# Chunked attention run by pairs of heads on the two halves of the TensorE array, its first pairs between the query products

## The chip, the cores and the metric

The kernel runs on one core of one Trainium2 chip. The metric is the device time of one execution in microseconds (us). Before the change three runs gave 1208.13, 1211.26 and 1212.42 us, median 1211.26. One further execution was profiled; its trace is what this document reads. About 0.3% (3.6 us) is what a measurement of this kernel can tell from no change.

The engines are named as the profile names them: PE is TensorE's matmuls, PEld its weight loads, DVE VectorE, ACT ScalarE, POOL GpSimd, SP the engine that issues the weight loads from memory.

## What is computed

Two blocks of two layers each on a sequence of 256 tokens of width 1024, all in float32. The change touches the attention of the second block's second layer, and two small places of the other two attentions:

```
def chunked_mixer(h, k_band, v_band, w_q, rel_table, w_o):
    q = (h @ w_q).reshape(B, n_c, CHUNK, B_HEADS, B_HEAD_DIM)      # 16 heads of 64
    ...
    s = jnp.einsum('bnqhd,bnkhd->bnhqk', q, k_band, preferred_element_type=jnp.float32)
    s = s * (B_HEAD_DIM ** -0.5) + bias[None, None]
    ...
    p = jax.nn.softmax(s, axis=-1).astype(v_band.dtype)
    o = jnp.einsum('bnhqk,bnkhd->bnqhd', p, v_band).reshape(B, S, B_HEADS * B_HEAD_DIM)
    return o @ w_o
```

It is followed by `x = x + rms_norm_2(y, attn_post_g)`, another norm, and the gated MLP of 2816 columns. The order of the whole is: attention with 8 heads of 128 (called `moba` in the kernel), MLP, pooling layer, MLP, latent attention with 8 heads (`mla`), gated MLP, shared keys and values, chunked attention with 16 heads (`chk`), gated MLP.

## The kernel before

**Weights.** Every weight matrix is cut into chunks of 128 x 2048 (1 MB). `AT` gives the first chunk of each matrix: `bq` are the four of the chunked attention's query weights, `bwo` the four of its output weights, `ffn1` those of the gated MLP behind it. There are four slots. For each chunk, in order: SP loads it (`raw`), ACT rounds it (`whi`, line 596, `hi_part`), DVE subtracts (`wlo`, line 854, `lo_part`), PE uses it. `hi_part` waits until PE is done with the chunk that was last in the slot (`w_used` above `PREV`). A product is three matmuls, on lines 1306, 1307 and 1308: rounded by rounded, and each rounded part by the other's rest. Activations are split in the same way into `act_hi` (ACT) and `act_lo` (DVE).

**Order.** Each engine has one program, written out by hand; semaphores tie them together. `hi_before(c)` and `lo_before(c)` convert all chunks whose slot was last held by a chunk before `c`. Inside the attention loop the function `due` says after which head one whole chunk is converted.

**Chunked attention.** First the four chunks of the query product, `tiles_out` into PSUM banks 4 and 5 in turn, 48 matmuls each, copied and scaled by DVE (line 1282) to `qT`. Heads 2j and 2j+1 lie in rows 0 to 63 and 64 to 127 of `qT[:, j]`. Then `attention(chk, ...)` goes head by head. On PE, for head h:

- **scores**: two matmuls (128 and 256 keys, line 1705) that use the 64 rows of one head, into bank 4 or 5; each is carried out as two instructions;
- **turn**: head h-2's probabilities are transposed, three matmuls into bank 6 (line 1428);
- **values**: head h-3, two matmuls (lines 1443 and 1444) that fill 64 columns of the array, into one half of the partitions of bank 7;
- **output**: from h = 5 on, half of one pair's output product (`head_out`, one token tile): six matmuls of 128x512. Banks 0 and 1 gather the first token tile, 2 and 3 the second.

DVE takes the maximum (`tensor_tensor_reduce`, line 1014, with the bias added), ACT the exponential (line 652), DVE normalizes (line 1027), ACT copies the transposed probabilities (line 640) and the head outputs (line 646), DVE splits them (line 1034, semaphore `o_lo`). `keep_busy` puts matmuls on constants between the first heads (`BUSY[chk]` = 1, 2, 1, 5), as it does in the phases in which PE waits for a norm. POOL loads each head's bias from memory and multiplies it by 8 (line 491); heads 8 to 15 reuse the buffers of heads 0 to 7, one after the other, once DVE has taken their maxima.

**The end of an attention.** The last two pairs' output products are made together by `rows_out`, 24 matmuls, quarter by quarter. After two quarters the first token tile is complete: `post_stats` has ACT sum its squares (line 609), then DVE scales (line 983) and adds it to x (line 987), multiplies by the next gain (line 942), and PE transposes the result (`turn("fpre1")`, line 1342).

## Time and profile before

| | us |
|---|---|
| three runs | 1208.13, 1211.26, 1212.42; median 1211.26 |
| the profiled execution, its own time | 1212.48 |
| its span, first to last instruction | 1210.7 |
| PE busy | 1154.4 (95%) |
| DVE busy | 676.7 (56%) |
| ACT busy | 530.9 (44%) |

The time of an execution is the span and 1.8 us around it. "PEclk" is the clock granted to TensorE as a share of full speed: 1.00 is 2.4 GHz, 0.50 is 1.2 GHz. The profile models the ends of matmuls, so that two following matmuls overlap on paper; how long a row of matmuls takes is read from start to start. The chain of work follows the last instruction back to whatever released it, and so tells which engine sets the time in each stretch.

### The profile page before, as it was taken

The numbers are of one execution on the slowest core, as the hardware profiler recorded it, in microseconds if no ns is written. First come the engines' busy times: TensorE is split into PE (matmuls) and PEld (weight loads), VectorE is DVE, ScalarE is ACT, GpSimd is POOL, SyncE is SP. The second block draws the span as 40 slices with busy tenths as digits, with TensorE's granted clock in tenths as the row PEclk, the third lists the DMA queues.
The fourth block names the chain that finished last, engine by engine and source line by source line (L and its number), as shares of the span: only waits on it lengthen the run. The fifth ranks groups of instructions, "written<-read, shape, count | busy, mean of one in ns | idle before, by whom it ended". The sixth has DMA issues, their size and how long they took to land.

```text
span 1210.7 us, 17821 instructions
## 1 busy us (share of the span) xinstructions
PE 1154.4 (95%) x7132; PEld 1019.1 (84%) x7132; DVE 676.7 (56%) x933; ACT 530.9 (44%) x640; POOL 43.5 (4%) x69
## 2 busy tenths in 40 slices
PE   4999899999999999997898999999999999999997
PEld 4887799999889999977677999999888668999996
DVE  4745554455665544566545655555845556554554
ACT  5446344344443443444444443345433455344342
POOL 0000000000000000000000000002300410000000
PEclk9999999999999999998899999999999899999999
DMA  9751445645535556455313565556653222556550
GB/s 350 250 186 56 154 158 189 207 169 178 191 99 195 170 190 205 145 136 191 105 35 104 174 195 180 180 191 209 207 191 136 62 91 66 178 174 200 181 173 35
DMA packets 127450, 196.37 MB, mean 162 GB/s; under 512 B 7392, under 2 KB 97632, under 8 KB 127280
## 3 DMA queue, kind: packets, MB, share of 16 engines
q1 hardware_dynamic: 124256, 186.29, 46.6%
q0 software_dynamic: 3152, 9.51, 2.6%
q8 instruction: 28, 0.46, 0.2%
q14 instruction: 14, 0.11, 0.0%
HBM read 194.73 MB, written 1.05 MB: 162 GB/s over the span
## 4 chain that ended last, share of the span: by engine, by line
PE 84%; DVE 10%; ACT 3%; issue 1%; DMA 1%; DVEq 0%; SPq 0%; ACTq 0%
PE ps L1306 26%; PE ps L1307 25%; PE ps L1308 25%; DVE wlo L854 2%; DVE xs L942 1%; ACT whi L596 1%; PE ps L1443 1%; PE ps L1705 1%; PE ps L1428 1%; ACT junk L609 1%; DMA raw<-attn_w_qkv_in 1%; DVE act_lo L956 1%; PE ps L1664 1%; PE ps L1328 1%; DVE x L987 1%
## 5 line engine op out<-in xcount | busy, mean ns | idle before, releaser
L854 DVE TENSOR_TENSOR wlo<-raw,whi 128x2048 fp32r<-128x2048 f32 (+2 forms) x176 | 395.9, 2266 | 182.1 <-ACT whi L596 181.7
L1306 PE MATMUL ps<-act_hi,whi 128*128 128x256 f32 x1384 | 392.6, 284 | 7.7 <-DVE act_lo L956 4.7
L1307 PE MATMUL ps<-act_lo,whi 128*128 128x256 f32 x1384 | 391.7, 283 | 0.0
L1308 PE MATMUL ps<-act_hi,wlo 128*128 128x256 f32 x1384 | 391.6, 283 | 0.0
L596 ACT ACTIVATE whi<-raw 128x2048 fp32r<-128x2048 f32 (+2 forms) x176 | 328.8, 1888 | 118.6 <-PE ps L1308 104.0
L1306 PEld LDWEIGHTS ps<-act_hi,whi 128*128 128x128 f32 x1384 | 263.6, 190 | 12.5 <-issue 9.6
L1307 PEld LDWEIGHTS ps<-act_lo,whi 128*128 128x128 f32 x1384 | 263.6, 190 | 2.0
L1308 PEld LDWEIGHTS ps<-act_hi,wlo 128*128 128x128 f32 x1384 | 263.7, 191 | 0.0
L1308 PE MATMUL ps<-whi,hlo 128*128 128x512 f32 x400 | 156.8, 392 | 0.0
L1307 PE MATMUL ps<-wlo,hhi 128*128 128x512 f32 x400 | 156.8, 392 | 0.0
L1306 PE MATMUL ps<-whi,hhi 128*128 128x512 f32 x400 | 156.2, 390 | 0.0
L1306 PE MATMUL ps<-whi,act_hi 128*128 128x512 f32 (+2 forms) x286 | 112.8, 394 | 9.2 <-DVE act_lo L956 5.5
L1307 PE MATMUL ps<-wlo,act_hi 128*128 128x512 f32 (+2 forms) x286 | 109.1, 381 | 0.0
L1308 PE MATMUL ps<-whi,act_lo 128*128 128x512 f32 (+2 forms) x286 | 108.9, 381 | 0.0
L1053 DVE TENSOR_TENSOR arena<-arena 128x512 f32<-128x512 f32 x32 | 22.2, 692 | 132.4 <-ACT arena L668 132.4
L1308 PEld LDWEIGHTS ps<-whi,hlo 128*128 128x128 f32 x400 | 75.2, 188 | 16.0
L668 ACT ACTIVATE arena<-ps 128x512 f32<-128x512 f32 x32 | 19.1, 598 | 156.3 <-PE ps L1308 156.3
L1306 PEld LDWEIGHTS ps<-whi,hhi 128*128 128x128 f32 x400 | 75.2, 188 | 14.7
L1307 PEld LDWEIGHTS ps<-wlo,hhi 128*128 128x128 f32 x400 | 75.1, 188 | 14.6
L1306 PEld LDWEIGHTS ps<-whi,act_hi 128*128 128x128 f32 x286 | 54.7, 191 | 21.5 <-issue 8.3
L1308 PEld LDWEIGHTS ps<-whi,act_lo 128*128 128x128 f32 x286 | 54.6, 191 | 10.1
L1307 PEld LDWEIGHTS ps<-wlo,act_hi 128*128 128x128 f32 x286 | 54.9, 192 | 8.5
(157 smaller groups left out, 906.6 us busy)
## 6 DMA issues: line engine op xcount, KB each, us to landing
raw<-mlp_w_up_in SPq DMA_DIRECT2D x32, 1024.0 KB, 6.3
raw<-mlp_w_down_in SPq DMA_DIRECT2D x32, 1024.0 KB, 4.9
raw<-ffn_w_gate_in SPq DMA_DIRECT2D x22, 1024.0 KB, 5.4
raw<-ffn_w_up_in SPq DMA_DIRECT2D x22, 1024.0 KB, 5.3
raw<-ffn_w_down_in SPq DMA_DIRECT2D x22, 1024.0 KB, 4.8
raw<-attn_w_qkv_in SPq DMA_DIRECT2D x12, 1024.0 KB, 8.6
raw<-w_kv_shared_in SPq DMA_DIRECT2D x8, 1024.0 KB, 6.7
raw<-attn_w_o_in SPq DMA_DIRECT2D x4, 1024.0 KB, 4.8
```

Of the source, the lines that this page charges most:

```text
L596: nc.scalar.activation(whi[:, s, 0:width], raw[:, s, 0:width], ACT.Copy).then_inc(hi_ready, 1)
L609: nc.scalar.activation(junk[:, col * HALF:col * HALF + width], src, ACT.Square, accum_out=norm_stat(name, t, 0, col, col + 1)).then_inc(sq ...
L668: nc.scalar.activation(relu, bank(4), ACT.Relu).then_inc(f.act_done, 1)
L854: nc.vector.tensor_tensor(wlo[:, s, 0:width], raw[:, s, 0:width], whi[:, s, 0:width].bitcast(F32), ALU.subtract).then_inc(lo_ready, 1)
L942: nc.vector.tensor_tensor(xs[:, t, cols], x[:, t, cols], row(name)[:, cols], ALU.mult)\
L956: nc.vector.tensor_tensor(act_quarter(act_lo, name, p), bank(4 + p).rearrange("p (k t) -> p k t", t=P), act_quarter(act_hi, name, p).bitca ...
L987: nc.vector.scalar_tensor_tensor(out=x[:, t, cols], in0=xs[:, t, cols], scalar=norm_stat(name, t, 6), in1=x[:, t, cols], op0=ALU.mult, op1 ...
L1053: nc.vector.tensor_tensor(hf, relu, relu, ALU.mult).then_inc(f.h_done, 1)
L1306: nc.tensor.matmul(dst, lhsT=left[0], rhs=right[0], start=start, stop=False, **kw)
L1307: nc.tensor.matmul(dst, lhsT=left[0], rhs=right[1], start=False, stop=False, **kw)
L1308: return nc.tensor.matmul(dst, lhsT=left[1], rhs=right[0], start=False, stop=stop, **kw)
L1328: nc.tensor.matmul(bank(b, 0, T), lhsT=ident, rhs=const[:, C_BAND:C_BAND + T], start=True, stop=True)
```

## The change

1. **Pairs.** The chunked attention has a program of its own. `pair_scores` issues the scores of heads 2j and 2j+1 alternately (rows 0 to 63, rows 64 to 127), into banks 4 and 5. `pair_values` issues the values of both alternately (columns 0 to 63, columns 64 to 127 of the array), into the two halves of bank 7. `probs` gets a fourth buffer, `probsT` moves into `junk`.
2. **First pairs between query products.** The third and fourth query chunk go to banks 1 and 0, in two halves each, with the scores of pair 0 and pair 1 between the halves. The `keep_busy` matmuls of this attention are gone. The order of a later step on PE is: turn, half an output product, turn, half an output product, values, scores of the pair after next.
3. **Half chunks.** In steps 2 to 8 ACT converts half a chunk (`hi_half`), in steps 4 to 9 DVE does (`lo_half`), in place of `due`.
4. **The last output product.** In all three attentions `rows_out` at the end makes only the last pair's product (12 matmuls); the one before it is issued by `head_out` inside the loop, behind the last values. 

```diff
-def due(cursor, w_o, h, heads):
-
-
-    return PREV[cursor] < w_o + max(0, (h - 4) // 2 if heads == 8 else (h - 5) // 4)
+def due(cursor, w_o, h):
+
+
+    return PREV[cursor] < w_o + max(0, (h - 4) // 2)
...
-        probs = sb("probs", [P, 3, 3 * P])
-        probsT = sb("probsT", [P, 2, 3 * P])
+        probs = sb("probs", [P, 4, 3 * P])
+        probsT = junk[:, 0:6 * P].rearrange("p (a n) -> p a n", a=2)
...
+            def hi_half():
+
+                q = cursor[0]
+                s, n = SLOT[q], half_done[0]
+                if n == 0:
+                    act.wait_ge(w_loaded[s], 16 * NTH[q])
+                    act.wait_ge(w_used, PREV[q] + 1)
+                ins = nc.scalar.activation(whi[:, s, n * D:(n + 1) * D], raw[:, s, n * D:(n + 1) * D], ACT.Copy)
+                half_done[0] = 1 - n
+                if n:
+                    ins.then_inc(hi_ready, 1)
+                    cursor[0] += 1
...
+                if half_done[0]:
+                    hi_half()
+                    return
...
+            def pair_step(at, j):
+                for e in range(2):
+                    if j:
+                        copy_probs(at, 2 * (j - 1) + e)
+                    if j < KT:
+                        exponentials(at, 2 * j + e, 2 * (j % 2) + e)
+                if j == KT - 1:
+                    preload(ACT.Sqrt)
+                if j:
+                    copy_out(at, j - 1)
...
+            hi_before(AT["bq"] + 2)
+            pair_step(chk, 0)
             hi_before(AT["bq"] + 3)
-            attention(chk, AT["bwo"])
-            hi_before(AT["bwo"] + 2)
+            pair_step(chk, 1)
+            for j in range(2, KT + 1):
+                pair_step(chk, j)
+                hi_half()
+            hi_before(AT["bwo"] + 3)
...
+            def pair_maxima(at, j, masks):
+                for e in range(2):
+                    mask = masks(2 * j + e)
+                    dve.wait_ge(at.scored, j + 1)
+                    maxima(at, 2 * j + e, mask, 2 * (j % 2) + e, 4 + e)
+
+            def pair_normalized(at, j):
+                for e in range(2):
+                    normalized(at, 2 * j + e, 2 * (j % 2) + e)
...
+            for j in range(4):
+                lo_before(AT["bq"] + j)
+                if j >= 2:
+                    pair_maxima(chk, j - 2, biases)
+                copy_queries(j)
+                if j >= 2:
+                    pair_normalized(chk, j - 2)
+            for j in range(2, KT + 2):
+                split_out(chk, j - 2)
+                if j < KT:
+                    pair_maxima(chk, j, biases)
+                if j >= 4:
+                    lo_half()
+                if j < KT:
+                    pair_normalized(chk, j)
+            lo_before(AT["bwo"] + 3)
...
-                    moba: (0, 0, 2, 7), mla: (0, 0, 2, 1), chk: (1, 2, 1, 5)}
+                    moba: (0, 0, 2, 7), mla: (0, 0, 2, 1)}
...
-                if k == KT - 2:
-                    rows_out(slot(c), k, lambda k, t: acts(k, t * P, (t + 1) * P), False, True, final)\
+                if k == KT - 1:
+                    rows_out(slot(c), k - 1, lambda k, t: acts(k, t * P, (t + 1) * P), False, True, final, (1,))\
                         .then_inc(w_used, 1)
-                elif k < KT - 2:
+                else:
...
-                    k = (h - 5) // 2 if pairs else h - 4
-                    if 0 <= k < KT - 2:
+                    k = h - 4
+                    if 0 <= k < KT - 1:
                         pe.wait_ge(at.o_lo, k + 1)
-                        if pairs:
-                            head_out(w_o, k, final, ((h - 5) % 2,))
-                        else:
-                            head_out(w_o, k, final)
+                        head_out(w_o, k, final)
                 pe.wait_ge(at.o_lo, KT)
-                head_out(w_o, KT - 2, final)
+                head_out(w_o, KT - 1, final)
...
+            def pair_scores(at, score, j):
+
+
+                if j:
+                    pe.wait_ge(at.maxed, 2 * j)
+                for t in range(TT):
+                    lo, hi = (0, P) if t == 0 else (P, 3 * P)
+                    for e in range(2):
+                        ins = score(2 * j + e, t, bank(4 + e, lo, hi))
+                ins.then_inc(at.scored, 1)
...
+            def pair_values(at, value, j):
+                pe.wait_ge(at.p_copied, 2 * j + 2)
+                if j:
+                    pe.wait_ge(at.o_lo, j)
+                for b in range(2):
+                    for e in range(2):
+                        o = ps[64 * e:64 * (e + 1), 7 * HALF + b * P:7 * HALF + T]
+                        probs_in = probsT[:, e, 0:T] if b == 0 else probsT[:, e, T:3 * P]
+                        ins = nc.tensor.matmul(o, lhsT=value(2 * j + e, b), rhs=probs_in,
+                                               start=b == 0, stop=b == 1)
+                ins.then_inc(at.mixed, 1)
+
+            def pairs_from(at, first, score, value, w_o, final):
+
+                for j in range(first, KT + 1):
+                    k = j - 2
+                    for e in range(2):
+                        turn_pair(at, j - 1, e)
+                        if e == 0:
+                            pe.wait_ge(at.o_lo, k + 1)
+                        head_out(w_o, k, final, (e,))
+                    pair_values(at, value, j - 1)
+                    if j + 1 < KT:
+                        pair_scores(at, score, j + 1)
+                pe.wait_ge(at.o_lo, KT)
+                head_out(w_o, KT - 1, final)
...
+            pe.wait_ge(vs_copied, 2)
+            pe.wait_ge(v_copied, 6)
+            for j in range(4):
+                c = AT["bq"] + j
+                wait_chunk(c + 1)
+                if j < 2:
+                    tiles_out(slot(c), 4 + j, "pre1" if j == 0 else None).then_inc(w_used, 1)
+                    continue
+                tiles_out(slot(c), 3 - j, columns=(0,))
+                if j == 2:
+                    pe.wait_ge(qT_copied, 2)
+                pair_scores(chk, chunk_score, j - 2)
+                if j == 3:
+                    turn_pair(chk, 0, 0)
+                tiles_out(slot(c), 3 - j, columns=(1,)).then_inc(w_used, 1)
+            turn_pair(chk, 0, 1)
+            pe.wait_ge(qT_copied, 4)
+            pair_scores(chk, chunk_score, 2)
+            pair_values(chk, chunk_value, 0)
+            pairs_from(chk, 2, chunk_score, chunk_value, AT["bwo"], TILES)
```

Line 1395 to 1397 of the changed kernel are 1306 to 1308 of the one before, 1818 the scores (1705), 1501 the turn (1428), 1560 the values (1443, 1444), 612 the half conversion, 664 and 669 the two copies on ACT (640, 646), 627 the sum of squares (609).

PE in the chunked attention's loop, before: two heads, with one half output product each.

```order
L1705 MATMUL ps<-arena 128x128 [waits chk_maxed]
L1705 MATMUL ps<-arena 128x256
L1428 MATMUL ps<-const,probs 128x128 [waits chk_p_copied,chk_normed]
L1428 MATMUL ps<-const,probs 128x128 x2
L1443 MATMUL ps<-probsT,arena 64x256 [waits chk_o_lo,chk_p_copied]
L1444 MATMUL ps<-probsT,arena 64x128
L1306 MATMUL ps<-whi,act_hi 128x512 [waits lo_ready,chk_o_lo]
```

The same place in the changed kernel, from the second half output product of a step to the first of the next:

```order
L1397 MATMUL ps<-whi,act_lo 128x512
L1560 MATMUL ps<-junk,arena 64x256 [waits chk_o_lo,chk_p_copied]
L1560 MATMUL ps<-junk,arena 64x256
L1560 MATMUL ps<-junk,arena 64x128 x2
L1818 MATMUL ps<-arena 128x128 [waits chk_maxed]
L1818 MATMUL ps<-arena 128x128
L1818 MATMUL ps<-arena 128x256 x2
L1501 MATMUL ps<-const,probs 128x128 [waits chk_p_copied,chk_normed]
L1501 MATMUL ps<-const,probs 128x128 x2
L1395 MATMUL ps<-whi,act_hi 128x512 [waits lo_ready,chk_o_lo]
```

Both heads' values stand together, and both heads' scores behind them; the turns stand apart, each before half an output product.

ACT at the end of the chunked attention, before: the last two copies of probabilities and head outputs, then the squares of the first token tile.

```order
L640 ACTIVATE probsT<-ps 128x384 [waits chk_p_turned]
L646 ACTIVATE act_hi<-ps 128x256 [waits chk_mixed]
L640 ACTIVATE probsT<-ps 128x384 [waits chk_p_turned]
L646 ACTIVATE act_hi<-ps 128x256 [waits chk_mixed]
L609 ACTIVATE junk,stat<-ps 128x1024 [waits acc_part]
```

In the changed kernel:

```order
L590 ACT_TABLE_LOAD
L590 ACTIVATE table<-const 128x1
L669 ACTIVATE act_hi<-ps 128x256 [waits chk_mixed]
L612 ACTIVATE whi<-raw 128x1024
L664 ACTIVATE junk<-ps 128x384 [waits chk_p_turned] x2
L669 ACTIVATE act_hi<-ps 128x256 [waits chk_mixed]
L612 ACTIVATE whi<-raw 128x1024 [waits w_used,w_loaded1]
L627 ACTIVATE junk,stat<-ps 128x1024 [waits acc_part]
```

The seventh half conversion, of a chunk of the next MLP, now stands between the last head output and the squares; it waits for `w_used`.

## Rows read from the trace of the kernel before

**Rows 1.** The page: engine shares, and the chain that ended last, by engine.

```profile
PE 1154.4 (95%) x7132; PEld 1019.1 (84%) x7132; DVE 676.7 (56%) x933; ACT 530.9 (44%) x640; POOL 43.5 (4%) x69
...
PE 84%; DVE 10%; ACT 3%; issue 1%; DMA 1%; DVEq 0%; SPq 0%; ACTq 0%
```

**Rows 2.** PE, start of the chunked attention: start, us, line, shapes, count [idle before].

```profile
934.61 0.92 PE L1705 MATMUL ps<-arena 64*128 64x128 f32 x4 [0.78 <-DVE arena L1282]
...
943.66 4.28 PE L1328 MATMUL ps<-const 128*128 128x256 f32 x10
```

**Rows 3.** Busy us and count per engine, then PEclk: query products, start, its middle, later heads.

```profile
922.20:933.80 11.60, 11.60 (x97) 11.42 (x96) 5.97 (x4) 3.84 (x2) 0.00 (x0) 1.00 0.54 179
933.80:947.80 14.00, 13.22 (x39) 8.65 (x39) 8.01 (x31) 5.02 (x14) 4.40 (x5) 0.63 0.31 91
937.00:946.00 9.00, 9.00 (x24) 5.82 (x24) 6.51 (x25) 4.58 (x13) 4.22 (x5) 0.51 0.41 120
947.80:996.50 48.70, 48.70 (x230) 30.93 (x228) 25.31 (x108) 26.97 (x78) 14.25 (x20) 1.00 0.24 69
```

**Rows 4.** The chain, two later heads: start, us, engine, line.

```profile
958.60 0.85 PE ps L1705 x4
959.45 0.48 PE ps L1428 x3
959.93 0.57 PE ps L1443 x2
960.72 0.43 PE ps L1306
...
966.03 0.85 PE ps L1705 x4
```

**Rows 5.** The chain, last heads and what follows.

```profile
996.54 0.39 ACT act_hi L646
...
997.44 0.50 PE ps L1306
...
1000.49 1.12 ACT junk L609 x2
1001.87 1.13 DVE xs L983
```

**Rows 6.** ACT, between the last exponential and the last pair.

```profile
991.58 1.28 ACT L590 ACT_TABLE_LOAD   x1
```

**Rows 7.** PE, while the norm behind the chunked attention runs.

```profile
1003.01 1.89 PE L1328 MATMUL ps<-const 128*128 128x256 f32 x8
1005.47 0.66 PE L1342 MATMUL ps<-const,xs 128*128 128x128 f32 x4 [0.57 <-DVE xs L942]
...
1007.35 2.76 PE L1328 MATMUL ps<-const 128*128 128x256 f32 x12
1010.40 0.66 PE L1342 MATMUL ps<-const,xs 128*128 128x128 f32 x4 [0.29 <-DVE xs L942]
```

**Rows 8.** PEclk around PE's longest wait, behind the latent norms, and PE there.

```profile
557.00:559.00 2.00, 0.00 (x0) 0.00 (x0) 0.55 (x5) 1.63 (x6) 0.00 (x0) 0.83 0.95 389
...
567.00:569.00 2.00, 2.00 (x7) 1.54 (x7) 2.00 (x1) 0.00 (x0) 0.00 (x0) 0.61 0.52 137
...
560.71 2.34 PE L1342 MATMUL ps<-const,xs 128*128 128x128 f32 x8 [5.56 <-DVEq L1213]
```

**Rows 9.** ACT, conversion of a whole chunk, 955 to 990: busy us, mean ns.

```profile
L596 ACT ACTIVATE whi<-raw 128x2048 fp32r<-128x2048 f32 x2 | 3.8, 1897 | 0.0
```

**Rows 10.** POOL: the first bias of head 8, its scaling, and that of head 15.

```profile
936.82 0.59 POOL L533 DMA_DIRECT2D arena<-b_rel_table_in  x1 [67.36 <-DVE soft L1018]
...
973.74 1.90 POOL L491 TENSOR_SCALAR arena<-arena 128x256 f32<-128x256 f32 x1 [2.24 <-DMA arena<-b_rel_table_in]
```

**Rows 11.** The chain at the end of the latent attention, then of the first.

```profile
647.44 1.12 ACT junk L609 x2
...
127.09 1.91 ACT whi L596
```

More of the change, by code:

```diff
@@ L1018, in attention @@
[L1018 to L1019 removed]
+                        maxima(at, h, mask, h % 3, 4 + h % 2)
                     g = h - 1
                     if 0 <= g < at.heads:
[L1022 to L1024 removed]
@@ L1352, in _, with rows_out @@
             TILES = [(h, t) for t in range(TT) for h in range(2)]
-            def rows_out(w, k0, left, first, last, final=None):
+            def rows_out(w, k0, left, first, last, final=None, rows_of=(0, 1)):
                 for n, (half, t) in enumerate(final or TILES):
-                    for k in range(2):
+                    for k in rows_of:
                         ins = product(bank(2 * t + half), left(k0 + k, t),
@@ L1365, in rows_out, with tiles_out @@
                 return ins
-            def tiles_out(w, b, enter=None):
-                for f in range(2):
+            def tiles_out(w, b, enter=None, columns=(0, 1)):
+                for f in columns:
                     for k in range(KT):
@@ L1405, in head_out, with turn_probs @@
                         ins.then_inc(w_used, 1)
+            def turn_probs(at, g, buffer):
+                pe.wait_ge(at.normed, g + 1)
+                if g >= 1:
+                    pe.wait_ge(at.p_copied, g)
+                for b in range(3):
+                    ins = nc.tensor.transpose(bank(6, b * P, (b + 1) * P),
+                                              probs[:, buffer, b * P:(b + 1) * P], ident)
+                ins.then_inc(at.p_turned, 1)
             def attention(at, score, value, w_o, final):
-                pairs = at.heads == 16
                 for h in range(at.heads + 3):
@@ L1692, in _ @@
             turn("pre1")
-            for j in range(4):
-                c = AT["bq"] + j
-                wait_chunk(c + 1)
-                if j >= 2:
-                    pe.wait_ge(qT_copied, j - 1)
-                tiles_out(slot(c), 4 + j % 2, "pre1" if j == 0 else None).then_inc(w_used, 1)
-            pe.wait_ge(qT_copied, 4)
-            pe.wait_ge(vs_copied, 2)
-            pe.wait_ge(v_copied, 6)
             def chunk_score(h, t, o):
```

141 lines of the change are left out of this document (76 added, 65 removed).

## The prediction

> **What bounds the kernel now.** I began with the page: PE is busy 95% of the span, DVE 56%, ACT 44%, and the chain of work that ended last lies on PE for 84% of the span and on DVE for 10% [rows 1]. So time is won where PE does less, or where it waits or runs at half clock. Next the windows of the chunked attention. Two chunks of the query product take 11.6 us, with PE full and the clock at 1.00. The 14 us behind them are the start of the attention: the mean clock is 0.63, and in 9 us of them 0.51, PE's lower level, 1.2 GHz [rows 3]. PE had waited 0.78 us for DVE's last copy of the queries, then ran scores of one head at a time, and before the clock came back it spent 4.28 us on ten instructions of `keep_busy`, which compute nothing [rows 2]. From 947.8 to 996.5 the clock is 1.00 and PE is never idle, while ACT is busy 27.0 us of 48.7 and DVE 25.3 [rows 3]. The chain there is PE alone. For one head it goes: scores 0.85, turn 0.48, values 0.79 (959.93 to 960.72), then half an output product; two heads take 7.43 us (958.60 to 966.03), so that product is the remaining 1.6 [rows 4]. At the end PE waits 0.94 us for the last copy and split (996.5 to 997.44), twelve matmuls complete the first token tile, and at 1000.49 the squares start; from there the chain is on ACT and DVE [rows 5]. So what counts is when ACT can start those squares.
>
> **Values and scores in pairs.** An instruction on 256 columns takes 0.23 us (twelve in 2.76) [rows 7]. A head's scores are two of these and two half as long, 0.66, and about 0.2 for the change of shape makes the 0.85 [rows 4]. Values likewise, 0.66 and 0.13. If the second head's instructions run while the first head's second one still does, a pair needs the time of eight short instructions instead of twelve: 0.88 + 0.2 = 1.1 for scores, 1.05 for values, 2.15 together. The trace has no two halves side by side, so the bounds: 1.64 if the second head is free (0.85 + 0.79), 3.28 if it costs as much as alone; one after the other, but in one burst, is 2.95. I take 2.15, as the two heads share neither rows (scores) nor columns (values) and write other banks or partitions.
>
> The Trainium skill bears on this (TensorE: Matmul & The Clock Gate, section "What overlaps and what doesn't"): weight loads overlap running matmuls only where the row groups differ. By that rule the value halves, on the same 128 rows, would gain nothing. The busy sums speak against it as it stands: in the query products PE's matmuls and its weight loads are both busy for over 11.4 of 11.6 us, all on the same rows [rows 3].
>
> **The new stretch, step by step**, from 922.2 (end of the second query chunk, the same in both):
> - Query products 11.6 [rows 3]. Between them two pairs' scores 2.2 and the first pair's turns 0.96 (the second behind them). The wait for the last query copy was 0.78 [rows 2]; the turn covers half, 0.35 is left.
> - Scores of pair 2 and values of pair 0, 2.15, a turn 0.48, then PE waits for the first split: 0.94 as at the end [rows 5], less the turn, 0.5. That is 940.5.
> - Half an output product: twelve matmuls take 3.05, the first 0.50 [rows 5], so six lie between 1.4 and 1.6; behind a turn I take 1.45. The step of pair 2 from there: 1.45 + 0.48 + 1.45 + 2.15 = 5.5. Four full steps of 0.96 + 2.9 + 2.15 = 6.0, against 7.43: 24.0. The step without scores: 4.9. That is 974.9.
> - Step 8. ACT now loads the square root's table (1.28) [rows 6] ahead of the copy of pair 6, which PE needs. I reckon 1.2 of wait behind the turn; 0.48 + 1.2 + 1.45 + 0.48 + 1.45 + 1.05 = 6.1. Then 0.94 of wait and 3.05 for twelve matmuls [rows 5]: the last product ends at 985.0. Before, the first token tile was ready at 1000.5, with another 2.8 us of product behind it.
> - **The seventh half conversion.** It belongs to the third chunk of the next MLP, whose slot was held by the last output chunk (by `place`); so it waits for `w_used` of the last product and stands ahead of the squares on ACT. `rows_out` is now one pair's product: six matmuls complete the first tile, six more the second, and I have counted all twelve. Then comes half of 1.897 us [rows 9], 0.95. The squares start at 986.0 instead of 1000.5: **14.5 us won**. Without that conversion they could start 2.4 us earlier, behind six matmuls.
>
> The other work fits below. ACT and DVE have the same work as before in about three quarters of the time, so some 75% of it. POOL's chain of biases runs from the first maximum (936.8) to 975.6, 39 us for eight heads [rows 10]. The first scores now end near 926.2 (922.2 + 2.9 + 1.1) and DVE has a conversion in front of the maximum, so it starts near 927.5 and ends near 966.5; the last pair's maxima are due near 970 and have a step of slack. The other half conversions find their slots free. SP's loads wait for DVE's conversions, which follow ACT's by two steps.
>
> **The other two attentions.** In the first, the chain behind the last values is a whole conversion on ACT (1.91) [rows 11], DVE's conversion behind it and then the residual; PE's order doesn't touch it: 0. In the latent one the squares wait for the first tile [rows 11]: it was 0.94 + twelve matmuls behind the last values and is now eighteen, the first twelve in place of the wait. 18 x 0.23 + 0.3 = 4.4 against 4.0: **0.4 lost**.
>
> **The clock behind the change.** After the last product PE has `keep_busy` for 1.89 us and then waited 0.57 for the first turn, which came 5.0 us after the squares began [rows 5, 7]. Now PE is done about when the half conversion starts, so the squares end later against PE: the first turn comes 0.95 + 5.0 behind the last product, and 6.0 - 1.9 = 4.1 us of idle stand there. The nearest row is an idle stretch of 5.56 us: the granted clock went from 1.00 to 0.50 about 3 us in, and came back some 8 us after PE resumed [rows 8]. At half clock the twelve instructions between the second and third turn take 5.5 us instead of 2.76, and they had only 0.3 to spare (PE waited 0.29 for the third turn) [rows 7]. So the third turn and all behind it is late by about 2.5: **2.5 lost**, which I take as the likelier case. If the clock holds, it is 0.
>
> **Sum.** 14.5 - 0.4 - 2.5 = 11.6. Against the profiled execution, 1212.48, that makes 1200.9. The median of the runs shown is 1.2 below that execution, so such a median would be 1199.7; I give 1200.9.
>
> **Rivals.**
> - **The clock holds in the norm.** 4.1 us of idle is less than 5.56. Then 1198.4. Chance 0.2.
> - **The halves go one after the other.** 2.95 instead of 2.15 per pair, eight times 0.8: 6.4 more, 1207.3. Only the values may do so: 8 x 0.4 = 3.2 more, 1204.1. For it: the first instruction after each change of shape is slower (0.43 and 0.50 against 0.23) [rows 4, 5], and the new order changes halves three times in a burst. Against it: such a burst comes half as often. Twice the price of one head (3.28) would give 1209.9. Chance 0.2 in all, 0.06 of it for the values alone. (The Trainium skill's rule above would make it the values alone.)
> - **The clock falls at the start again.** PE waits twice there, 0.35 and 0.5, with scores and values between, and in the trace the fall came behind a wait of 0.78 [rows 2]. 9 us at half [rows 3] are 4.5 lost: 1205.4. Against it: dense products reach to 936, and two heads at once fill the array. Chance 0.12.
> - **Slower.** One mechanism: the clock falls near 937, as it did near that place before, and with no `keep_busy` left in this attention it stays at half. Each us of PE's work then costs one more; from 937 to 985 there are some 45. After 14 us of such work, 28 us of time, the gain of 14.1 is gone; to the end of the attention it would be 1243. Against it: at 947.8 scores, turns and values alone followed each other at 1.00 [rows 3]. Chance 0.03.
> - **Nothing happens**, as ACT's squares wait for something else: excluded, the squares wait for PE's tile today [rows 5].
>
> **The numbers.** The forecast has 0.45. The low end, 1195, takes the clock as holding and pairs nearly at 1.64 (1198.4 less 8 x 0.5 would be 1194.4). The high end, 1208.5, takes in the halves one after the other and the clock at the start. About 0.3%, 3.6 us, is what a measurement here can tell: all cases but the last, and the sum of two bad ones (above 1208.9), are faster by more. So 0.93 faster, 0.04 the same, 0.03 slower.
>
> **What would show it.** In the profile after: pairs of scores and values at 2.1 us a pair, step to step 6.0; PEclk near 1.00 from 937 to 985; ACT's half conversion starting where PE's last product ends, and the squares behind it, at 986; PE idle some 4 us behind that with the clock at 0.50 near 990; in the latent attention the squares 0.4 later against the last values. It is wrong if a pair takes 3 us, if the clock is low in the attention, or if the squares start before the last product ends.

## The result and the profile after

The changed kernel takes **1193.41 us** (median of four runs, 1193.38 to 1194.76). Before it was 1211.17 (four runs, 1208.13 to 1212.42). The ratio is 0.986, with a 95% interval of 0.9843 to 0.9878: faster by 1.2 to 1.6%. The prediction said 1200.9, with a range of 1195.0 to 1208.5. So the direction is right, but the gain is 7.5 us larger than forecast and the time lies 1.6 us below the range. The profiled execution took 1193.40 us with a span of 1191.6; the one before took 1212.48 with 1210.7 [rows 1]. The spans differ by 19.1 us.

The page of the changed kernel: busy us per engine, the granted clock in 40 slices, the chain that ended last by engine.

```profile
PE 1132.8 (95%) x7114; PEld 1008.9 (85%) x7114; DVE 677.9 (57%) x936; ACT 531.0 (45%) x644; POOL 41.9 (4%) x69
...
PEclk9999999999999999998979999999999998999999
...
PE 84%; DVE 9%; ACT 4%; issue 1%; DMA 1%; DVEq 0%; SPq 0%; ACTq 0%
```

DVE and ACT do the same work as before [rows 1]. PE is busy 21.6 us less, more than the span's 19.1, and still for 95%: none of the gain is idle time, which grew by 2.5. It is fillers, half clock and heads that ran one after the other.

The stretch has to be measured inside one trace, since what lies ahead of it differs by up to 3.4 us between executions of programs that are the same up to there (the first mark below stands at 661.15 in e5, at 664.56 in e4; more on this at the end). I use two marks: the first product of the MLP behind the latent attention, and the first product of the MLP behind the chunked one. Before they stand at 660.99 and 1014.03, **353.04 us** apart; after at 661.29 and 994.96, **333.67 us**. So the stretch between them gains 19.37, and the 0.30 by which the first mark is later (0.14 of it is already there at the latent attention's first score) makes up the rest of the 19.1. This length is called "the stretch" below.

Changed kernel, stages of the chunked attention and the norm behind it (columns as in rows 3: busy us and count per engine, then PEclk, DMA share, GB/s):

```profile
922.50:937.00 14.50, 14.32 (x119) 13.15 (x118) 10.71 (x31) 7.22 (x16) 3.73 (x5) 1.00 0.51 159
937.00:946.00 9.00, 8.26 (x57) 5.75 (x58) 6.43 (x31) 6.26 (x19) 3.85 (x6) 1.00 0.13 26
946.00:965.00 19.00, 19.00 (x123) 13.51 (x121) 15.60 (x65) 14.75 (x45) 8.63 (x13) 1.00 0.29 82
965.00:980.00 15.00, 13.03 (x75) 9.53 (x74) 7.98 (x23) 8.13 (x19) 0.75 (x2) 1.00 0.35 108
981.70:986.00 4.30, 0.02 (x1) 0.00 (x0) 3.47 (x10) 1.66 (x5) 0.00 (x0) 0.89 0.18 74
986.00:990.00 4.00, 3.98 (x14) 3.38 (x15) 3.79 (x10) 1.29 (x3) 0.00 (x0) 0.50 0.00 0
990.00:995.00 5.00, 5.00 (x25) 4.17 (x23) 4.21 (x8) 1.24 (x3) 0.00 (x0) 0.81 0.00 0
```

From 937 to 946 the clock is 1.00, where it had been 0.51 [rows 3]; it holds through the attention. Then PE is idle for 4.3 us, and the clock falls to 0.50, as forecast.

Changed kernel, the chain in one full step: start, us, engine, line.

```profile
943.32 0.80 PE ps L1560 x8
944.12 0.86 PE ps L1818 x8
...
948.56 0.80 PE ps L1560 x8
949.36 0.86 PE ps L1818 x8
950.22 0.48 PE ps L1501 x3
...
952.08 0.33 PE ps L1501 x3
```

This is the row to keep. The values of two heads (L1560, eight instructions with their loads) take 0.80 us, the scores of two heads (L1818) 0.86. Before, one head's values took 0.79 and one head's scores 0.85 [rows 4]. **The second head costs nothing.** A step is 5.24 us (944.12 to 949.36); two heads had taken 7.43.

Changed kernel, the chain at the end of the attention:

```profile
968.68 0.87 ACT probs L657 x4
969.57 1.28 ACT L590
971.07 0.28 ACT act_hi L669
971.37 0.44 DVE act_lo L1087
971.85 0.50 PE ps L1395
...
976.08 0.39 ACT act_hi L669
976.49 0.44 DVE act_lo L1087
976.97 0.50 PE ps L1395
...
980.09 1.06 ACT whi L612
981.15 1.01 ACT junk L627 x2
```

The table load stands ahead of the copy that PE waits for (until 971.85), the last copy and split cost 0.94 as before, and then ACT converts half a chunk (1.06) before the squares, which start at 981.05 instead of 1000.49 [rows 5]. (The chain counts them only from 981.15, where the conversion is over by its count; 981.05 is the start of ACT's own row.)

### The profile page after: what moved, and what is told of

It is laid out like the page before. It is cut to its first block, busy times and chain, and to the rows that moved or that the text cites. A ratio compares the mean times of both kernels' runs of the same rounds, so it can differ in the third digit from the quotient of the medians.

```text
span 1191.6 us, 17784 instructions
## 1 busy us (share of the span) xinstructions
PE 1132.8 (95%) x7114; PEld 1008.9 (85%) x7114; DVE 677.9 (57%) x936; ACT 531.0 (45%) x644; POOL 41.9 (4%) x69
## 4 chain that ended last, share of the span: by engine, by line
PE 84%; DVE 9%; ACT 4%; issue 1%; DMA 1%; DVEq 0%; SPq 0%; ACTq 0%
PE ps L1395 26%; PE ps L1397 26%; PE ps L1396 26%; DVE wlo L895 2%; ACT whi L596 1%; DVE xs L1001 1%; ACT junk L627 1%; DMA raw<-attn_w_qkv_in 1%; PE ps L1501 1%; PE ps L1787 1%; PE ps L1785 1%; DVE act_lo L1015 1%; PE ps L1417 1%; DVE x L1046 1%; DVE xs L1042 1%
## 5 line engine op out<-in xcount | busy, mean ns | idle before, releaser
L895 DVE TENSOR_TENSOR wlo<-raw,whi 128x2048 fp32r<-128x2048 f32 (+2 forms) x173 | 389.1, 2266 | 178.9 <-ACT whi L596 177.8
L596 ACT ACTIVATE whi<-raw 128x2048 fp32r<-128x2048 f32 (+2 forms) x172 | 321.2, 1888 | 114.1 <-PE ps L1397 99.4
L704 ACT ACTIVATE arena<-ps 128x512 f32<-128x512 f32 x32 | 19.1, 598 | 156.3 <-PE ps L1397 156.3
```

The costliest lines, as they stand in the source:

```text
L596: nc.scalar.activation(whi[:, s, 0:width], raw[:, s, 0:width], ACT.Copy).then_inc(hi_ready, 1)
L704: nc.scalar.activation(relu, bank(4), ACT.Relu).then_inc(f.act_done, 1)
L895: nc.vector.tensor_tensor(wlo[:, s, 0:width], raw[:, s, 0:width], whi[:, s, 0:width].bitcast(F32), ALU.subtract).then_inc(lo_ready, 1)
```

## The experiments

Nine kernels ran. The first three edit the changed kernel at the points where the trace of after left the prediction's steps; e4 takes the early start back; e5 and e9 test why a pair is so cheap; e6 and e7 are versions for use; e8 is one part of the change alone on the kernel before.

| kernel | median us | the stretch us | against after |
|---|---|---|---|
| before | 1211.17 | 353.04 | +19.37 |
| after | 1193.41 | 333.67 | 0 |
| e1, heads of a pair one after the other | 1195.01 | 333.39 | -0.28 |
| e2, without the seventh half conversion | 1191.54 | 330.94 | -2.73 |
| e3, fillers in the norm | 1196.32 | 333.32 | -0.35 |
| e4, first pairs behind the queries | 1202.81 | 339.86 | +6.19 |
| e5, scores on the same rows | 1198.04 | 338.45 | +4.78 |
| e6, e2 and a late table load | 1191.07 | 330.37 | -3.30 |
| e7, e6 and fillers in the latent attention | 1185.00 | 330.39 | -3.28 |
| e8, before with the last product of after | 1214.08 | 353.72 | +20.05 |
| e9, values on the same columns | 1200.6 | 337.81 | +4.14 |

e5 and e9 stand here with one execution each; a second one of e5 took 2641.8 us, which nothing in its program accounts for, and is left out.

The stretch ends with the norm, and what half clock costs there is up to 0.37 us (e3). From the squares to the next product it is 13.91 us in after, but 13.53 in e1, e5 and e9, 13.54 in e2 and 13.68 in e4. So the attention itself is compared by the time from the first mark to the squares, 319.76 us in after: 0.10 more in e1, 2.36 less in e2, 6.42 more in e4, 5.17 more in e5, 4.52 more in e9.

**e1: the order inside a pair.** Scores and values of the first head are issued whole, then the second's.

```diff
-                for t in range(TT):
-                    lo, hi = (0, P) if t == 0 else (P, 3 * P)
-                    for e in range(2):
+                for e in range(2):
+                    for t in range(TT):
+                        lo, hi = (0, P) if t == 0 else (P, 3 * P)
...
-                for b in range(2):
-                    for e in range(2):
+                for e in range(2):
+                    for b in range(2):
```

> In the changed kernel both scores of a pair take 0.86 us and both values 0.80, as much as one head's took before (0.85, 0.79). Here the two heads of a pair are issued one after the other (both matmuls of head 2j, then both of head 2j+1), for scores and for values; same matmuls, same banks, same waits. Theory A (the halves of the array work at the same time, and only where neighbouring instructions belong to different halves): scores rise to 1.3 to 1.5 and values to 1.25 to 1.45, a step from 5.25 to about 6.2 to 6.45, eight times 1.0 to 1.2: 8 to 9.5 us slower than the changed kernel, about 1202. Rival B (a pair is cheap because it stands in one burst with one change of shape, or the engine overlaps whatever is queued): scores and values stay under 1.0 each, at most 2 us slower.

The chain of e1, one step:

```profile
946.23 0.81 PE ps L1560 x8
947.03 0.86 PE ps L1818 x8
```

0.81 and 0.86, and up to the squares 0.10 us more than after (the stretch's 0.28 less is the norm): the order of issue doesn't matter. That left two readings: the two heads run at once because they lie on different halves of the array, or any such burst is cheap.

**e5: scores of both heads on the same rows.**

```diff
             def chunk_score(h, t, o):
-                lo = 64 * (h % 2)
+                lo = 0
```

> The changed kernel, but chunk_score takes rows 0 to 63 of queries and keys for both heads of a pair (the odd heads' scores are then computed from the even heads' rows: that part of the result is another one, the number and size of the instructions are the same). Theory A: the pair's scores take 0.86 us because its two heads lie on different row halves of the array and run at once; on the same half they go one after the other, twelve short units of 0.11 and 0.2 for the change of shape = 1.5 us a pair, 0.65 more, in eight pairs 5.2 us more between the latent attention's first output-side product and this attention's (333.67 us in the kernel after), total near 1198.6; values stay at 0.80. Rival B: the halves have nothing to do with it, a burst of small instructions costs this little in any case: scores stay at 0.86 and the time at 1193.4.

The chain of e5, one step:

```profile
945.12 0.80 PE ps L1560 x8
945.93 1.50 PE ps L1818 x8
```

1.50, to the hundredth what twelve short units and the change of shape make, with the same instructions of the same size. The stretch is 4.78 longer, and 5.17 up to the squares, where eight times 0.64 are 5.1. The values, untouched, stay at 0.80.

**e9: values of both heads on the same columns.** Both heads of a pair have the same 128 rows here, and differ only in the columns that they fill.

```diff
-                        o = ps[64 * e:64 * (e + 1), 7 * HALF + b * P:7 * HALF + T]
+                        o = ps[0:64, 7 * HALF + e * T + b * P:7 * HALF + (e + 1) * T]
```

(with the order of e1).

> The changed kernel, but in pair_values the odd head's outputs go to the same partitions 0 to 63 as the even head's, in other columns of the bank, one head after the other (e1 showed that this order alone changes nothing: 0.81 us). The rows 64 to 127 that ACT copies then hold old data, so the odd heads' outputs are left out of the result; number and size of the instructions are the same. Theory A: values cost 0.80 us a pair because the two heads use different column halves and run at once, though they use the same rows; on the same columns they go one after the other, twelve short units of 0.11 and 0.13 = 1.45, 0.65 more, some 5 us in the stretch of 333.67 (scores on the same rows: 1.50 and 4.8 more). Rival B (the rule by which only different rows overlap): columns have no part in it, and 0.80 stays.

The chain of e9, one step:

```profile
947.01 1.44 PE ps L1560 x8
948.45 0.86 PE ps L1818 x8
```

1.44 instead of 0.80, and the stretch is 4.14 longer (4.52 up to the squares, where eight times 0.64 are 5.1). So the halves of the array work at once in both directions: rows for the scores, columns for the values. Rival B fell in e5 and in e9.

**e2: the seventh half conversion.** ACT converts no half chunk in the last step; that chunk is converted behind the squares, in its turn.

```diff
                 pair_step(chk, j)
-                hi_half()
+                if j < KT:
+                    hi_half()
```

> ACT's seventh half conversion, which waits for the last product, is left out of the attention; the whole chunk is converted in the next MLP, as before the change. Theory A (the squares are on the path and wait for it): the squares start about 2.5 us earlier against the last values (at about 978.5 where they started at 981.05), PE's idle stretch behind the attention shrinks from 4.3 to about 1.8 us, the kernel is 2.5 to 2.8 us faster, about 1190.8. Rival B (the whole conversion in the next MLP is late for PE there): 0 to 1 us faster, with a wait of PE for wlo in the first 12 us of the MLP.

ACT in e2 (start, us, instruction, idle before):

```profile
976.14 0.38 ACT L669 ACTIVATE act_hi<-ps 128x256 fp32r<-128x256 f32 x1 [1.72 <-PE ps L1561]
978.73 1.03 ACT L627 ACTIVATE junk<-ps 128x1024 f32<-128x1024 f32 x1 [2.21 <-PE ps L1398]
```

The squares come 3.51 us behind the last values (975.22 to 978.73) instead of 5.89, and the stretch is 2.73 shorter, 2.36 of it ahead of the squares. The conversion was on the path, and with it the wait for all twelve matmuls instead of six.

**e3: the clock in the norm.** Twelve filler instructions instead of four in the gap (`"fpre1": (12, 1, 6, 1, 2)`).

> The changed kernel with 12 instead of 4 filler matmuls ahead of the first turn of the norm behind the chunked attention (5.5 us at full clock, which ends before the turn is due), so that PE isn't idle for 4.3 us and the granted clock should stay at 1.00. My prediction (a late third turn is passed on in full): 2.0 to 2.5 us faster, about 1191. The theory after the trace (the third turn's lateness is covered, as DVE splits the first two turned tiles only behind its last gain product, and the third split comes after these): third turn back at 9.9 us behind the squares, but the first product of the MLP only 0.3 us earlier: 0.3 us faster, 1193.1.

PE in e3, while the norm runs:

```profile
989.27 0.66 PE L1431 MATMUL ps<-const,xs 128*128 128x128 f32 x4 [0.85 <-DVE xs L1001]
...
991.15 2.76 PE L1417 MATMUL ps<-const 128*128 128x256 f32 x12
994.21 0.66 PE L1431 MATMUL ps<-const,xs 128*128 128x128 f32 x4 [0.30 <-DVE xs L1001]
...
997.84 0.36 PE L1395 MATMUL ps<-act_hi,whi 128*128 128x256 f32 x1 [0.72 <-DVE act_lo L1015]
```

and the same place in the changed kernel:

```profile
986.01 1.12 PE L1431 MATMUL ps<-const,xs 128*128 128x128 f32 x4 [4.30 <-DVE xs L1001]
...
988.63 4.38 PE L1417 MATMUL ps<-const 128*128 128x256 f32 x12
992.85 0.60 PE L1431 MATMUL ps<-const,xs 128*128 128x128 f32 x4
...
994.96 0.36 PE L1395 MATMUL ps<-act_hi,whi 128*128 128x256 f32 x1
```

With the gap filled the clock stays at 1.00 and the third turn comes 9.91 behind the squares instead of 11.80. Yet the first product comes only 0.37 sooner behind the squares (13.54 against 13.91): in e3 PE then waits 0.72 for DVE's `act_lo`, in after it does not wait. Half clock on PE cost a third of a microsecond, because DVE was late anyway. e2 says the same without a filler: its idle stretch was 1.93 us, the clock fell (0.66 from 985 to 990), its third turn was 1.2 late, and its first product came 13.54 behind the squares, as with the clock held. e3's total is the higher one for what lies ahead of the stretch: its first mark stands 3.23 us later than after's, 1.58 of it already at the latent attention's first score, the rest behind a longer half-clock stretch there (e7).

**e4: the early start taken back.** All query products stand first, then the scores and turns of the first two pairs; DVE and ACT in the order that goes with it.

```diff
-                pair_scores(chk, chunk_score, j - 2)
-                if j == 3:
-                    turn_pair(chk, 0, 0)
...
+            pair_scores(chk, chunk_score, 0)
+            pair_scores(chk, chunk_score, 1)
+            turn_pair(chk, 0, 0)
+            turn_pair(chk, 0, 1)
```

> The changed kernel with the scores of the first two pairs and the first turns behind all query products instead of between them, so that nothing of PE's covers the first maxima, exponentials and normalizations. Theory A (the place between the products hides the latency of the first pairs and keeps the clock up): the values of pair 0 come some 5 us later, PE waits about 5 us in pieces near 935 to 943, and the clock falls to 0.50 there, another 2 to 4.5 us: 1199 to 1203. Rival B (the place is worth only the waits): the clock stays at 1.00 and it is 3 to 5 us slower, 1196.5 to 1198.5. Rival C (the gain at the start came from leaving out the filler matmuls and from pairs): under 1 us slower.

PE in e4 at the start of the attention, and two windows (columns as in rows 3):

```profile
940.16 0.93 PE L1816 MATMUL ps<-arena 64*128 64x128 f32 x8 [1.91 <-DVE soft L1071]
...
942.34 0.52 PE L1499 MATMUL ps<-const,probs 128*128 128x128 f32 x3 [0.67 <-ACT junk L664]
943.66 0.93 PE L1816 MATMUL ps<-arena 64*128 64x128 f32 x8 [0.81 <-DVE soft L1071]
...
935.00:945.00 10.00, 6.58 (x54) 4.75 (x55) 6.97 (x32) 4.59 (x18) 2.97 (x5) 1.00 0.07 12
945.00:985.00 40.00, 36.86 (x222) 26.20 (x220) 27.55 (x111) 27.68 (x77) 13.37 (x21) 0.96 0.32 87
```

DVE and PE in e4 ahead of its last step:

```profile
975.81 0.29 DVE L1067 CUSTOM_DVE_ANT_0 probs<-ps,arena 128x128 f32<-128x128 f32 x1 [2.44 <-POOL arena L491]
...
978.50 0.55 PE L1499 MATMUL ps<-const,probs 128*128 128x128 f32 x3 [1.75 <-DVE probs L1080]
```

The stretch is 6.19 longer. PE is busy for 6.58 of the first 10 us and waits for the rest, mostly for DVE's softmax statistics; the clock stays at 1.00 there. But this is only half of the loss. Counted from the first mark, the first output product comes 3.1 us later than in after (946.33 against 939.95), and it stays at that up to the values of pair 6. Then DVE waits 2.44 us for the last pair's bias, as POOL's chain of biases begins only at 939.55 here (928.00 in after) and takes its time; PE waits 1.75 for the turn behind it, where it did not wait at all in after. Behind that wait and the next one of 0.93 the clock falls, PEclk is 0.58 from 980 to 984, and by the last values the delay is 6.4. So the early start is worth 6.2 us as a whole: about 3.1 of latency hidden at the start, and 3.3 because it gives POOL's biases their cover, without which a wait of 1.75 and a half-clock stretch of some 1.6 follow. The median of 1202.81 lies in theory A's 1199 to 1203, but not by A's way: at the start the clock held and 3.1 us were lost, as B said.

**e8: the last output product alone**, on the kernel before.

```diff
-                if k == KT - 2:
-                    rows_out(slot(c), k, lambda k, t: acts(k, t * P, (t + 1) * P), False, True, final)\
+                if k == KT - 1:
+                    rows_out(slot(c), k - 1, lambda k, t: acts(k, t * P, (t + 1) * P), False, True, final, (1,))\
```

> The kernel before with one part of the change alone: in all three attentions the last output product behind the last values is one pair's rows instead of two, what came before goes in the regular places (12 instructions ahead, 12 instead of 24 behind). By the trace of after, in the latent attention the squares came 4.53 us behind the last values instead of 4.36, so 0.15 more there; in the chunked attention the twelve instructions moved ahead take 2.9 us and fill the wait of 0.94, and six instead of twelve stand ahead of the first tile's squares (1.4 less): 2.9 - 0.94 - 1.4 = 0.5 more; in the first attention nothing. Together 0.7 more, 1211.9 against 1211.2, no difference that can be measured. Rival: the product spares half of its work behind the end, so the attention's turns come 1.4 us sooner: 1209.8.

In the stretch 0.68 more (353.72 against 353.04), all of it ahead of the squares, where 0.5 was expected. From the latent attention's last values to the next first product it is 18.11 against 17.91, 0.20 more, where 0.15 was expected. The ratio to before is 1.0015 (0.9994 to 1.0036), no measurable difference; the median in the table is the higher one in part for what lies ahead, as the profiled execution's first score in the latent attention stands 1.1 us later than before's (595.96 against 594.84). This part of the change wins nothing.

**e6: two repairs together.** e2, and ACT loads the square root's table behind the last copy of outputs; also more fillers in two norms (7 and 8 instead of 4).

```diff
-                if j == KT - 1:
-                    preload(ACT.Sqrt)
                 if j:
                     copy_out(at, j - 1)
+                if j == KT:
+                    preload(ACT.Sqrt)
```

> A version for use: the changed kernel without the seventh half conversion in the attention, with the square root's table loaded behind ACT's last copy of attention outputs, and with keep_busy of 7 in place of 4 in the norm behind this attention and 8 in place of 4 in the norm behind the latent one. From the runs so far: 2.7 us for the conversion (measured alone: 2.73 in the stretch), 0.5 for the table load (it held the copy of pair 6 by 1.02 behind a turn of 0.48, and only 0.5 of wait is left without it), 0.3 for the clock in the norm: 3.5 less, 1189.9. Rival: ACT loads the table behind the last copy in the way of the squares (1.28 us, with 0.94 + 2.9 us of PE's work to hide it: it fits), so no gain of it: 1190.4. If the conversion is only put off and held up something later, 1193.

PE and ACT in e6 at the end of the attention:

```profile
972.48 0.50 PE L1396 MATMUL ps<-whi,act_hi 128*128 128x512 f32 x1 [0.47 <-DVE act_lo L1088]
...
977.10 1.28 ACT L590 ACT_TABLE_LOAD   x1
...
979.29 1.03 ACT L627 ACTIVATE junk<-ps 128x1024 f32<-128x1024 f32 x1 [0.69 <-PE ps L1398]
```

The wait behind the copy of pair 6 is 0.47 instead of 1.02, and the load fits behind PE's six matmuls: ACT still waits 0.69 for them before the squares. The stretch is 0.57 shorter than e2's, all of it the table load; the fillers in this norm gave nothing more (13.55 from squares to product, as e2). The median is 1191.07, below after's 1193.41 though not by the whole 3.3. In the profiled execution the missing 1.2 lies ahead of all that was changed: the latent attention's first score stands at 596.16 instead of 594.98.

**e7: fillers in the latent attention's waits.**

```diff
                 if j:
+                    pe.wait_ge(qn_copied, 4)
+                    keep_busy(3, 7)
                     pe.wait_ge(kn_copied, 2)
...
             pe.wait_ge(qn_copied, 4)
+            keep_busy(3, 7)
             pe.wait_ge(qrT_copied, 2)
```

> The kernel of e6 and, ahead of the latent attention, three instructions of keep_busy in each of PE's two waits of 1.47 us (at 586 and 593), behind which the granted clock fell to 0.50 near 596 in every trace and came back after about 5 us in some executions and later in others (PEclk from 600 to 615 was 0.67 in the kernels before and after, 0.50 in e1, e3 and e4; those took 1.7 us longer from the first score to the last values). Theory A: the fall comes of these waits; with them filled the clock is 1.00 from 590 to 615 and the attention's 48.2 us from first score to last values become some 43 to 45: 3 to 5 us less than e6, about 1186, and the second level 3 us higher goes away. Rival B: the clock falls for the thin work itself (scores of one head at a time, with waits between), fillers ahead of it don't matter: the time of e6. Rival C: the fillers stand in the way of the scores: up to 1.5 us slower than e6.

Windows from 600 to 615 in after, in e1 and in e7 (columns as in rows 3). After:

```profile
600.00:610.00 10.00, 10.00 (x25) 5.85 (x23) 5.06 (x17) 4.05 (x10) 0.00 (x0) 0.52 0.34 102
610.00:615.00 5.00, 5.00 (x26) 3.53 (x26) 2.55 (x14) 2.00 (x7) 0.00 (x0) 1.00 0.03 8
```

e1:

```profile
600.00:610.00 10.00, 10.00 (x25) 5.93 (x24) 5.05 (x17) 4.51 (x13) 0.00 (x0) 0.50 0.26 85
610.00:615.00 5.00, 5.00 (x14) 3.23 (x14) 1.43 (x8) 0.75 (x3) 0.00 (x0) 0.51 0.12 42
```

e7:

```profile
600.00:610.00 10.00, 10.00 (x47) 6.63 (x48) 7.45 (x29) 6.33 (x19) 0.00 (x0) 1.00 0.33 107
```

The half-clock stretch is gone: from the latent attention's first score to its last values it is 42.06 us instead of 48.23 in e6 and in after (49.87 in e1). The median is **1185.00 us** (1183.46 to 1185.29), 0.9786 of before (0.9771 to 0.9802), 6.1 below e6. This is the fastest version. Theory A held, and gave somewhat more than its 3 to 5.

## Why the prediction was right and wrong

**Right in kind.** PE's own work sets the attention's length, the start before the last query products, the clock that holds there, the seventh conversion on the path, idle time in the norm and a fallen clock behind it: all came as the steps said. Four sizes were off. By the prediction's steps:

- **Values and scores in pairs: 2.15 forecast, 1.66 measured.** This is the step that failed most. I took "the second head's instructions run while the first head's second one still does", eight short instructions. In fact the halves run at once throughout, which was the named lower bound of 1.64. The trace of before could not have shown it: its last two heads' values do follow each other, but the second head's started only at 995.64, when ACT had copied its probabilities. Eight pairs times 0.49 are **3.9 us**. e5 and e9 show the reason, and the size with both halves occupied one after the other (1.50 and 1.44): the rival's 2.95 was the right price for heads on the same half. The Trainium skill's rule (TensorE: Matmul & The Clock Gate, "What overlaps and what doesn't") is on weight loads, which overlap running matmuls only where the row groups differ. The scores, with different rows, fit it. Taken at its word it would leave no overlap for the values, on the same 128 rows, as the second head's weights could only be loaded behind the first head's matmuls; the trace has 0.80 for the two heads on different columns and 1.44 on the same ones, so here the measurement decides against this sentence. It is one sentence of the page, and the prediction did not draw on what the page has on packing by columns.
- **Turns and half products: 0.96 + 2.9 forecast, 3.6 measured.** I took both turns at 0.48. Only the first of a step, behind scores, costs that; the second, behind a product, 0.33 (the row at 952.08 above), and the half products take 1.39, not 1.45. About 0.27 in each of six or seven steps: **1.5 to 2 us**. The rows that I had picked have a turn only behind scores [rows 4]. The chain of before had the other price too, in the two last steps without scores, where a turn stands behind a product (again at 994.73):

```profile
992.01 0.33 PE ps L1428 x3
```

So this part could have been read beforehand.
- **The start.** 18.3 from the end of the second query chunk to the first output product was forecast (922.2 to 940.5), 17.3 measured (922.64 to 939.95). The two waits were forecast as 0.35 and 0.5 and measured as 0.46 and 0.47; the 1.0 between is the cheaper pairs again, part of the 3.9. The clock held.
- **Step 8 and the end.** The wait behind the table load was 1.02 (forecast 1.2), the last one 0.94 as forecast, the half conversion 1.06 (0.95). The squares started at 981.05, forecast 986.0.
- **The clock behind the change: 2.5 lost forecast, 0.3 measured.** The mechanism came true: 4.3 us of idle (4.1 forecast), the clock at 0.50 from 986 to 990, the third turn late by 1.9 (11.80 behind the squares, 9.91 before). Wrong was the sentence that all behind it is late by the same. I had read the cover on the third turn alone (0.29 of wait [rows 7]). But the first product waits for DVE's splits, and DVE issues these in order behind its four gain products: the first split starts 11.5 us behind the squares both before (1012.00) and after (992.55), whether the third turn comes 9.91 or 11.80 behind them. e3 and e2 show it: with the clock held, PE waits 0.72 for `act_lo`. **2.2 us** of the miss.
- **The latent attention.** 0.4 lost forecast. The squares came 0.17 later behind the last values (4.53 against 4.36). There too PE was idle (1.94 us) and the clock fell to 0.50 from 655 to 657, which I had not foreseen, and cost nothing at the first product for the same reason. e8 gives 0.20 for this part alone.
- **Covers.** POOL's last bias was scaled by 965.15, a microsecond ahead of the last pair's first maximum (966.12). No wait for it or for a chunk's load shows on the chain. How thin that cover is shows in e4, where it was gone.

The sum of the misses: 5 us at the squares (3.9 for the pairs, 1.5 for turns and products, 0.2 in step 8, less 0.4 by which the marks ahead already stood later and 0.1 for the conversion), 2.2 for the clock and 0.2 in the latent attention are 7.4, and 1200.9 less 7.4 is 1193.5.

**The range.** Its low end put the two best cases together, the clock holding and the pairs nearly at 1.64, which gave 1194.4. Both came about as far as the time goes, and the turns were cheaper by another 1.5 to 2 us. Those had been given one price without bounds, though the trace of before has two for the turn, 0.48 and 0.33.

**What each part is worth**, by taking it back in the changed kernel: early first pairs 6.2 (e4), scores on two row halves 4.8 (e5), values on two column halves 4.1 (e9). With the 2.7 that the seventh conversion costs (e2) and the 0.7 of the last product (e8), 19.4 + 2.7 + 0.7 - 15.1 = 7.7 us are left for the rest: `keep_busy` and half clock at the start gone, and fewer changes of shape per head. Counted up to the squares, without the norm's clock, it is 6.7. That remainder was not tried by itself, and parts taken back one at a time need not add up: of e4's 6.2 about half comes of POOL and the clock at the attention's end.

## What to carry to other kernels

Where two independent pieces of work each fill half of the array, by rows or by columns, put them side by side in one burst: the second was free here, in either order of issue (fp32, 64 rows or 64 columns each). When such a gain shortens a loop, look at the chains beside it: POOL's biases had a microsecond left here, and where it was gone (e4) a wait and half clock of 3.3 us together followed. Before you price a late or slowed engine, follow its product to the consumer and ask what that consumer is waiting for in its own queue: 1.9 us of delay became 0.3 here. Short PE waits of 1 to 2 us ahead of thin work are worth filling when the clock falls behind them; in this kernel two such waits cost 6 us, as much as the early start of the whole attention won.

## What the runs showed of the hardware that I had not expected

- **Column halves work at once** with the same rows and different weights: 0.80 us for two heads, 1.44 on the same columns (e9), at fp32 tiles of 128 by 64.
- **The total time moves with the clock in places that the change doesn't touch.** Behind the two waits of 1.47 us the clock fell near 596 in every trace without fillers there, but came back at different times: PEclk from 610 to 615 is 1.00 in after and 0.51 in e1, with the same program up to there. That is 1.64 us (48.23 against 49.87). Another 1.24 stand ahead of it (first score at 594.98 and at 596.22), and 0.8 of these are there at 139 us already: at the very first products, from 22 to 26, PEclk is 1.00 in after and 0.70 in e1. This is why e1 and e3 look slower than after while their stretch is shorter. It may be why the single runs of before lie between 1208.1 and 1213.4, but one of them alone has a trace, and the mean granted clock on record for each doesn't settle it (0.983 both at 1208.93 and at 1213.35). Filling the waits took 6.1 us off; whether it also steadies the time isn't shown (e7's five runs span 1.8 us, e6's five 3.2, after's four 1.4). What decides how long a stretch lasts stays open. A single run of e8 took 1203.0, 11 below its median: its mean clock is 0.992 against 0.978 to 0.985 in the others, so it spent less time at half clock, but no trace of it shows where.
- **The length of a wait alone doesn't tell whether the clock falls.** It fell behind an idle stretch of 1.93 us in e2 (PEclk 0.66 from 985 to 990). In e8 PE is idle for the same 1.93 us at the same place of the same norm, and the clock stays at 1.00 from 1004 to 1014:

```profile
1007.48 0.66 PE L1342 MATMUL ps<-const,xs 128*128 128x128 f32 x4 [1.93 <-DVE xs L942]
```

It did not fall in e3 and e6 either, where fillers left waits of 0.85 and 0.64. What else decides stays open.
